# Stick-breaking attention: the cumulative sums of softplus as full fp32 products in place of products of its two fp32r parts

## The reference

```python
z = jnp.einsum('bhtd,bhsd->bhts', qb, kb) * scale
strict = s_idx < t_idx
log_1m = jnp.where(strict, jax.nn.log_sigmoid(-z), 0.0)
suffix = lax.cumsum(log_1m, axis=3, reverse=True) - log_1m
a = jnp.where(strict, jnp.exp(jax.nn.log_sigmoid(z) + suffix), 0.0)
outs.append(jnp.einsum('bhts,bhsd->bhtd', a, vb))
```

## Time and profile before

| | us |
|---|---|
| median of 3 runs (2352.71, 2352.88, 2356.16) | 2352.88 |
| the profiled execution's own time | 2355.29 |
| its span in the trace | 2354.0 |
| PE busy | 2319.3 (99%) |
| DVE busy | 1065.6 (45%) |
| ACT busy | 907.5 (39%) |
| POOL busy | 1086.6 (46%) |

### The profile page before, as it was taken

One profiled execution on the slowest core, in us unless ns is written; L12 is line 12 of the kernel. 1 busy time (PEld: TensorE's weight loads), 2 busy tenths in 40 slices (PEclk: granted clock), 3 DMA queues, 4 the chain that ended last, 5 costly groups with the idle time before them and its releaser, 6 DMA issues.

```text
span 2354.0 us, 31502 instructions
## 1 busy us (share of the span) xinstructions
PE 2319.3 (99%) x12981; PEld 1988.0 (84%) x12981; DVE 1065.6 (45%) x1543; ACT 907.5 (39%) x1347; POOL 1086.6 (46%) x812
## 2 busy tenths in 40 slices
PE   8999999999999999999999999999999999999997
PEld 6767888888888988778888888889999999999886
DVE  3147755622210614867465222117676446754403
ACT  4324643522222425945434222225344334322321
POOL 5423844444455452048335444554445444544452
PEclk9999999999999999999999999999999999999999
DMA  4211422223232242324123322333211222232332
GB/s 164 90 63 63 160 73 75 96 90 99 91 107 99 97 132 77 87 82 160 63 72 99 99 94 95 100 98 114 66 45 64 90 91 89 90 98 90 99 99 72
DMA packets 69055, 219.69 MB, mean 93 GB/s; under 512 B 9840, under 2 KB 14064, under 8 KB 68912
## 3 DMA queue, kind: packets, MB, share of 16 engines
q1 hardware_dynamic: 64160, 214.26, 28.2%
q10 hardware_dynamic: 4752, 3.42, 0.5%
HBM read 207.29 MB, written 2.10 MB: 89 GB/s over the span
## 4 chain that ended last, share of the span: by engine, by line
PE 92%; DVE 5%; ACT 2%; issue 1%; DMA 1%; SPq 0%; DVEq 0%; ACTq 0%
PE ps L439 74%; PE ps L558 6%; PE ps L935 2%; PE ps L973 1%; PE ps L719 1%; PE ps L743 1%; PE ps L633 1%; DVE x L1687 1%; PE ps L880 1%; PE ps L836 1%; DMA w_land<-in_units 1%; PE ps L852 1%; PE ps L857 1%; DVE acc L1766 1%; PE ps L463 1%
## 5 line engine op out<-in xcount | busy, mean ns | idle before, releaser
L2413 POOL TENSOR_TENSOR w_lo<-w_land,w_hi 128x512 fp32r<-128x512 f32 x768 | 1045.7, 1389 | 1151.8 <-ACT w_hi L1070 1151.2
L439 PE MATMUL ps<-u_hi,w_hi 128*128 128x512 f32 (+3 forms) x2360 | 754.8, 346 | 13.1 <-DVE u_lo L1666 12.7
L439 PE MATMUL ps<-u_lo,w_hi 128*128 128x512 f32 (+3 forms) x2360 | 751.0, 344 | 0.0
L439 PE MATMUL ps<-u_hi,w_lo 128*128 128x512 f32 (+3 forms) x2360 | 748.4, 343 | 0.0
L1070 ACT ACTIVATE w_hi<-w_land 128x1024 fp32r<-128x1024 f32 x384 | 400.8, 1050 | 249.2 <-DMA w_land<-in_units 246.4
L439 PEld LDWEIGHTS ps<-u_hi,w_hi 128*128 128x128 f32 x2360 | 420.3, 188 | 76.4 <-DVE u_lo L1666 15.1
L439 PEld LDWEIGHTS ps<-u_lo,w_hi 128*128 128x128 f32 x2360 | 417.8, 188 | 56.4 <-issue 1.2
L439 PEld LDWEIGHTS ps<-u_hi,w_lo 128*128 128x128 f32 x2360 | 418.4, 188 | 54.9
L439 PE MATMUL ps<-hid_hi,w_hi 128*128 128x512 f32 (+1 forms) x594 | 220.2, 371 | 0.0
L439 PE MATMUL ps<-hid_lo,w_hi 128*128 128x512 f32 (+1 forms) x594 | 219.7, 370 | 0.0
L439 PE MATMUL ps<-hid_hi,w_lo 128*128 128x512 f32 (+1 forms) x594 | 219.4, 369 | 0.0
(11 more groups left out here) (354 smaller groups left out, 3244.2 us busy)
## 6 DMA issues: line engine op xcount, KB each, us to landing
w_land<-in_units SPq DMA_DIRECT2D x384, 512.0 KB, 3.4
x<-in_xT SPq DMA_DIRECT2D x4, 528.0 KB, 7.0
arena<-in_memT ACTq DMA_DIRECT2D x2, 1024.0 KB, 6.1
outT<-x SPq DMA_DIRECT2D x16, 128.0 KB, 1.7
sb_split<-sb_split SPq DMA_DIRECT2D x14, 128.0 KB, 2.5
sb_q_lo<-sb_q_lo SPq DMA_DIRECT2D x13, 128.0 KB, 2.3
sb_split<-sb_q_lo SPq DMA_DIRECT2D x8, 128.0 KB, 3.0
sb_k_lo<-sb_split SPq DMA_DIRECT2D x6, 128.0 KB, 3.1
```

The costliest lines, as they stand in the source:

```text
L439: ins = pe.matmul(ps[:, bank, at:at + c1 - c0], w, rhs(k, c0, c1)[which], start=first and h == 0, stop=last and h == 2)
L2413: pool.tensor_tensor(w_lo[:, u % LAND, half], w_land[:, u % LAND, half], w_hi[:, u % RING, half].bitcast(F32), ALU.subtract).then_inc(*uni ...
```

## The change

`sums` multiplies the plain fp32 softplus in `sp_` by fp32 views of the two constant matrices, one product where there were two. `upper` and `lower` and their tiles go; `value` signals PE itself. In `sums`, PE's wait for chunk 1 moves ahead of the products of minus ones into block 0; it stood behind them.

```diff
-        sp_hi, sp_lo = halves("sp_hi", 8192, 2, SPAN), halves("sp_lo", 16384, 2, SPAN)
...
-        neg_ones, neg_suffix, ident_r = (sums_c[:, n * P:(n + 1) * P] for n in range(3))
+        neg_ones, neg_suffix = (sums_c[:, n * P:(n + 1) * P].bitcast(F32) for n in range(2))
+        ident_r = sums_c[:, 2 * P:3 * P]
...
                 def sums(h, i):
                     at = 2 * i + h
-                    pe.wait_ge(*sb_lo_at.at(2 * at + 1))
+                    pe.wait_ge(*sb_sp.at(2 * at + 1))
                     for b in (3, 2, 1, 0):
+                        if b == 0:
+                            pe.wait_ge(*sb_sp.at(2 * at + 2))
                         for j in range(3, b, -1):
-                            for part in (sp_hi, sp_lo):
-                                pe.matmul(block(h, b, (j - b) * P), neg_ones, part[:, h, SB_AT[j]:SB_AT[j] + S - j * P],
-                                          start=False, stop=False, skip_group_check=True)
-                        if b == 0:
-                            pe.wait_ge(*sb_lo_at.at(2 * at + 2))
-                        for part in (sp_hi, sp_lo):
-                            ins = pe.matmul(block(h, b), neg_suffix, part[:, h, SB_AT[b]:SB_AT[b] + S - b * P],
-                                            start=False, stop=part is sp_lo, skip_group_check=True)
+                            pe.matmul(block(h, b, (j - b) * P), neg_ones, sp_[:, h, SB_AT[j]:SB_AT[j] + S - j * P],
+                                      start=False, stop=False, skip_group_check=True)
+                        ins = pe.matmul(block(h, b), neg_suffix, sp_[:, h, SB_AT[b]:SB_AT[b] + S - b * P],
+                                        start=False, stop=True, skip_group_check=True)
...
                 def softplus(h, i):
...
+                    for n, (a, z_) in enumerate(SB_PART):
+                        v = sp_[:, h, a:z_]
                         dve.wait_ge(*sb_ab.at(2 * (2 * i + h) + n + 1))
-                        dve.scalar_tensor_tensor(v, scores(h, n), 0.0, v, ALU.max, ALU.add).then_inc(*dve_own.up())
-
-                    def upper(n):
-                        own()
-                        dve.tensor_copy(chunk(n)[1], chunk(n)[0]).then_inc(*dve_own.up())
-
-                    def lower(n):
-                        v, hi, lo = chunk(n)
-                        dve.tensor_tensor(lo, v, hi.bitcast(F32), ALU.subtract).then_inc(*sb_lo_at.up())
-                    value(0)
-                    upper(0)
-                    value(1)
-                    own()
-                    lower(0)
-                    upper(1)
-                    own()
-                    lower(1)
+                        dve.scalar_tensor_tensor(v, scores(h, n), 0.0, v, ALU.max, ALU.add).then_inc(*sb_sp.up())
```

More of the change, by code:

```diff
@@ L364, in build @@
         hid_at, silu_at, hid_hi_at, hid_lo_at, conv_at = (sem(n) for n in ("hid", "gate_act", "hid_hi", "hid_lo", "gate_conv"))
-        sb_split, sb_stacked, sb_c, sb_ab, sb_lo_at, sb_a0, sb_a = (
-            sem(n) for n in ("sb_split", "sb_stacked", "sb_consts", "sb_log1p", "sb_lo", "sb_weights0", "sb_weights"))
+        sb_split, sb_stacked, sb_c, sb_ab, sb_sp, sb_a0, sb_a = (
+            sem(n) for n in ("sb_split", "sb_stacked", "sb_consts", "sb_log1p", "sb_softplus", "sb_weights0", "sb_weights"))
         mix_gam, mix_exp, mix_sig, mix_clip, mix_log, mix_pool, mix_g, mix_scaled, mix_gated = (
@@ L2119, in softplus @@
                 def softplus(h, i):
[L2121 to L2126, removed]
-                        dve.wait_ge(*sb_ab.at(2 * (2 * i + h) + n + 1))
-                        dve.scalar_tensor_tensor(v, scores(h, n), 0.0, v, ALU.max, ALU.add).then_inc(*dve_own.up())
-                    def upper(n):
-                        own()
-                        dve.tensor_copy(chunk(n)[1], chunk(n)[0]).then_inc(*dve_own.up())
-                    def lower(n):
-                        v, hi, lo = chunk(n)
-                        dve.tensor_tensor(lo, v, hi.bitcast(F32), ALU.subtract).then_inc(*sb_lo_at.up())
-                    value(0)
-                    upper(0)
-                    value(1)
-                    own()
-                    lower(0)
-                    upper(1)
-                    own()
-                    lower(1)
+                    for n, (a, z_) in enumerate(SB_PART):
+                        v = sp_[:, h, a:z_]
+                        dve.wait_ge(*sb_ab.at(2 * (2 * i + h) + n + 1))
+                        dve.scalar_tensor_tensor(v, scores(h, n), 0.0, v, ALU.max, ALU.add).then_inc(*sb_sp.up())
                 def out_lo(i):
```

## The result

The changed kernel takes 2375.53 us (median of 4 runs, 2374.61 to 2376.01) against 2353.84 for the kernel before (median of 4). The ratio is 1.009, 95% interval 1.0078 to 1.0102: slower by 18 to 24 us. The profiled execution took 2375.25 us.

What follows compares the result with a forecast made beforehand. PE was taken to bound the kernel's stage, ACT just behind. Dearer products, 23.8 us, less 4.3 hidden in idle time gave +19.5; on the median of 2352.88 that is 2372.4 us, range 2368 to 2378.

Steps and rivals of the forecast that it cites:

- The bound: PE bounds the stage, dense but for six waits for ACT, 3.5 us by modelled ends, with ACT just behind.
- The product: Sums on PE: ten plain fp32 products cost 4.33 us a head, 1.49 more than before, 23.8 us for 16 heads.
- the 2.84 that I took off: PE time in us of a head's old sums, taken for all 16 heads, with bounds of 2.76 and 2.88.
- rival D: Dearer products on PE, from kind changes (0.1 to 0.2 at 32 places) or 4.44 bound: +21 to +26 us; 8%.
- The idle time: PE's waits for ACT swallow 2.8 us in five turns and 1.49 at the first wait, together 4.3 us.
- its slot: ACT keeps the time of `weights(0, i, 0)`, which frees `z(0, i+1)` 3.38 us after the sums began.
- the second part of `z`: On PE, due 5.40 us after the sums began, ACT's weights ending at 5.10: no cost; if missed, 1 to 2 us.
- The loads: Old fp32r and full fp32 weight loads on PE both last 190 ns, so nothing was added.
- The moved wait and DVE: PE's earlier wait for softplus chunk 1 has 4 us of cover; DVE's removed 42 us are off PE's path: both nothing.
- The total: Whole kernel: +19.5 us on the earlier median of 2352.88 gives 2372.4 us, 0.83% slower, held at 80%.
- The clock term: HGRN stage: two 3.4 us stretches at clock 0.50 cost 1.7 us each; both may go or more may come.

## Why the prediction was right

**The bound.** PE's stream set the stage, and adding to it showed in full but for the waits. Right.

**The product.** I took 4.33 us a head from products of the mLSTM. The pitches were right (0.22, 0.43, 0.65 and 0.86 us for the four widths), and in the last head, behind a wide product, the sums take 4.34. Behind `z` they take 4.39 and behind `times_v` 4.44. Passing from one kind of product to the other costs nothing, as I had it: in the last head it happens too, and its first product is no dearer. What was mis-sized is the 2.84 that I took off. It was close to the mean of heads behind `z` and `times_v` (2.82 and 2.88), while 4.33 holds for a head behind a wide product, whose own sums took 2.77 before. Like for like a head grows by 1.56 to 1.57 and not by 1.49, in 16 heads 25.0 us and not 23.8. So rival D, dearer products from changes of kind, is not borne out.

I had also read that both kinds of 128-column product advance by 0.11 for each record. In the kernel before that holds only behind another narrow product. Behind a wider one the first of a pair takes 0.06, so the pair takes 0.17 where a full product takes 0.22:

```profile
956.20 0.22 PE L852 MATMUL ps<-sp_hi,sums_c 128*128 128x128 f32 x1
956.26 0.27 PE L852 MATMUL ps<-sp_lo,sums_c 128*128 128x128 f32 x1
956.37 0.33 PE L852 MATMUL ps<-sp_hi,sums_c 128*128 128x256 f32 x1
```

The sum did not suffer by it, as it took the old sums whole.

**The idle time.** 4.3 us were to be swallowed. By 25.0 less the 20.47 of the stage it was 4.5. Most of the rest is in `z`: behind an idle it took 1.74 us, and without one it takes 969.81 - 968.15 = 1.66. So the product was 1.2 us too low and the idle 0.2 to 0.3 too low, and the stage came out at +20.47 for +19.5; that the second error took off some of the first is luck. That the first wait and five turns swallow 0.40 each when only 0.40 is added is the finest test of the mechanism (+3.80 for +4.0). ACT kept its slot to 0.05 us, and the second part of `z`, costed at nothing, shows no wait.

**The loads.** The load of a plain matrix lasts 190 ns in the changed kernel as in the earlier trace rows, so nothing was lost there. In the changed turn loads are busy for 10.41 of 14.30 us, a smaller share than before (73% for 79%), while PE by starts has no room at all. Neither busy share tells this; the starts do.

Two rules stood beside these rows in the prediction, and neither shows in the runs. The Trainium skill (TensorE: Matmul & The Clock Gate, weight-path perf modes) has fast weight load on only where the type is not fp32. By the prediction's estimate from its factor of about two, that would have made the change 14 us worse than forecast. The Trainium skill (Perfetto Trace Analysis, identifying the most-contended engine) judges PE's room by load busy time, beside its share of peak arithmetic. By the load busy time PE had 21% to spare, and nothing would have changed.

**The moved wait and DVE.** Both at nothing, both shown at nothing by a run each. DVE is busy for 5.98 us in the turn (5.7 forecast).

**The total.** 2372.4 forecast, 2375.53 measured. 1.0 of the 3.1 us is the stage, 1.0 is the median of before, which moved from 2352.88 to 2353.84 with a fourth run; the rest, 1.1, lies outside the stage and within what repeated runs of one kernel differ by. The clock term was of the right kind: the changed kernel's profile has one low stretch in the HGRN stage where the earlier trace rows names one of two, and its time behind the stage is 1.5 us shorter. The run with one wait has none in that stage, and is 1.3 us shorter again (1327.55). Busy time of that stretch in the changed kernel:

```profile
1715.10:1718.50 3.40, 3.40 (x17) 0.50 0.17 34
```

What decides whether such a stretch comes is not settled here.

## What to carry to other kernels

Price a matrix product by the distance of starts of the same kind of product elsewhere in the trace, width by width: here two fp32r products of 512 columns cost 0.46 us and one full fp32 product 0.86, and only at 128 columns, behind another narrow product, do they cost the same 0.22. Take the two numbers that you subtract from the same place in the order of work: what stands ahead of a group moved its time by about 0.1 us here, in both kernels. Work taken off an engine that nobody waits for is worth nothing; check who is named as the releaser of the bound engine's waits before counting it. And when the bound engine is PE, what it saves can be lost to its clock: look at the granted clock of the stage before and after, and at who is next in line.

## What the runs showed that I had not expected

Half of PE's work for the sums was taken out, and nothing was gained, since 24 us of a stage of 118 ran at the 1.2 GHz level after PE had stood idle. Idle filled with useless products gave 6.4 us (2346.18 for 2352.62). In the profile of the kernel before, waits of 0.6 us a turn and 1.6 us at the start leave the clock at 1.00 throughout the stage, and they were also what took in 4.5 us of the change. With the two pairs merged the waits are only 0.1 us longer, and one stretch of 3.4 us at 0.50 came. Each is one profile, so where the clock begins to fall is not shown.
